# Which slots of a gather an expert's tokens take: dealt over eight groups of four, or filled in order

## The reference, cut to what matters

```python
scores = jax.nn.sigmoid((xf @ w_router).astype(jnp.float32))
...
_, top_idx = lax.top_k(jnp.where(expert_mask, sel_scores, -jnp.inf), TOP_K)
gates = jnp.take_along_axis(scores, top_idx, axis=-1)
gates = gates / gates.sum(-1, keepdims=True) * ROUTE_SCALE
...
hdn = jax.nn.silu(xb @ w_gate[e]) * (xb @ w_up[e])
return hdn @ w_down[e]
```

## Time and profile before

| | before |
|---|---|
| median of 3 runs (lowest, highest) | 1383.16 us (1380.08 to 1383.69) |
| the profiled execution's own time | 1383.16 us |
| its span in the profile | 1381.2 us |
| TensorE busy | 1340.4 us (97%) |
| SBUF loads and stores | 475.66 MB, 344 GB/s over the span |
| granted TensorE clock, mean | 0.993 of 2.4 GHz |

### The profile page before, as it was taken

How to read it: one execution, slowest core, us unless ns; L and a number is a source line. 1 busy time by engine, 2 the same in 40 slices (tenths; PEclk the granted TensorE clock), 3 DMA queues, 4 the chain that set the end, 5 groups by cost and what they waited for, 6 DMA issues and landing times.

```text
span 1381.2 us, 20332 instructions
## 1 busy us (share of the span) xinstructions
PE 1340.4 (97%) x7932; PEld 705.2 (51%) x7932; DVE 428.3 (31%) x1274; ACT 222.8 (16%) x551; POOL 356.9 (26%) x379
## 2 busy tenths in 40 slices
PE   8999999999999999999999999899999999999987
PEld 4755554455455455445447555454554545544443
DVE  0442563322322222222154424522223232232223
ACT  1154130111011010010121541201111111110001
POOL 2021345232232232222000212542322323222201
PEclk9999999999999999999999999999999999999999
DMA  9822468999999999999985224899999999999994
GB/s 330 327 94 90 153 232 318 423 418 421 421 421 418 422 422 421 420 422 421 414 290 200 91 109 154 304 377 420 420 417 421 421 420 419 422 422 420 421 425 194
DMA packets 92118, 475.66 MB, mean 344 GB/s; under 512 B 15165, under 2 KB 22553, under 8 KB 42769
## 3 DMA queue, kind: packets, MB, share of 16 engines
q1 hardware_dynamic: 76880, 442.73, 78.7%
q0 software_dynamic: 15168, 32.01, 6.4%
HBM read 491.21 MB, written 3.75 MB: 358 GB/s over the span
## 4 chain that ended last, share of the span: by engine, by line
PE 77%; SPq 10%; DMA 6%; DVE 3%; issue 1%; POOL 1%; ACT 1%; DVEq 0%; POOLq 0%; ACTq 0%
PE bank L692 26%; PE bank L721 13%; PE bank L661 13%; SPq L491 10%; PE bank L772 6%; DMA ring<-in_w_up_dram 5%; PE bank L783 5%; PE bank L999 3%; PE bank L894 1%; PE bank L657 1%; PE bank L1042 1%; PE bank L710 1%; PE bank L875 1%; PE bank L623 1%; PE bank L775 1%
## 5 line engine op out<-in xcount | busy, mean ns | idle before, releaser
L1985 POOL DMA_INDIRECT arena<-h_rows,rank_i x256 | 255.6, 999 | 608.0 <-DVE arena L1659 505.9
L692 PE MATMUL bank<-ring,arena 128*64 128x256 f32 x2784 | 314.9, 382 | 15.7 <-DMA ring<-in_w_up_dram 7.6
L692 PEld LDWEIGHTS bank<-ring,arena 128*64 128x64 f32 x2784 | 201.9, 138 | 139.0 <-issue 36.3
L661 PE MATMUL bank<-arena 128*128 128x512 f32 x512 | 247.1, 606 | 0.0
L1696 DVE TENSOR_TENSOR arena<-arena,bank 128x256 f32<-128x256 f32 x64 | 27.0, 421 | 560.6 <-ACT arena L1235 560.5
L721 PE MATMUL bank<-ring,arena 128*64 128x512 f32 x704 | 160.8, 598 | 0.0
L1640 DVE STREAM_TRANSPOSE arena<-arena 128x256 f32<-128x256 f32 x256 | 141.6, 610 | 25.9 <-DMA arena<-h_rows,rank_i 13.5
L692 PE MATMUL bank<-arena 128*64 128x256 f32 x1280 | 143.2, 379 | 3.0 <-DMA arena<-in_w_up_dram 1.9
L1240 ACT ACTIVATE arena<-bank 128x512 f32<-128x512 f32 x128 | 76.5, 597 | 430.4 <-PE bank L721 430.4
L661 PEld LDWEIGHTS bank<-arena 128*128 128x128 f32 x512 | 87.7, 191 | 88.9 <-issue 88.0
L692 PEld LDWEIGHTS bank<-arena 128*64 128x64 f32 x1280 | 91.7, 137 | 58.7 <-issue 10.3
(11 more groups left out here) (221 smaller groups left out, 904.4 us busy)
## 6 DMA issues: line engine op xcount, KB each, us to landing
ring<-in_w_up_dram SPq DMA_DIRECT2D x44, 2048.0 KB
ring<-in_w_down_dram SPq DMA_DIRECT2D x44, 2048.0 KB
ring<-in_w_gate_dram SPq DMA_DIRECT2D x43, 2048.0 KB
arena<-in_w_gate_dram SPq DMA_DIRECT2D x20, 2048.0 KB
arena<-in_w_up_dram SPq DMA_DIRECT2D x20, 2048.0 KB
arena<-in_w_down_dram SPq DMA_DIRECT2D x20, 2048.0 KB
ring<-in_w_in_dram SPq DMA_DIRECT2D x8, 2048.0 KB, 21.2
ring<-in_w_o_dram SPq DMA_DIRECT2D x4, 2048.0 KB, 11.9
```

The costliest lines, as they stand in the source:

```text
L661: last = mm(bank[SUM_BANKS[n][half]][0:w, :], selg[:, u, t0:t0 + w], y_sb[:, u, half * 512:(half + 1) * 512], start=False, stop=stop, skip ...
L692: last = mm(bank[5][64 * e:64 * e + 64, part * F:(part + 1) * F], xgT[:, u, kk, 64 * e:64 * e + 64], w[e][:, kk, :], start=(kk == 0), stop ...
L1985: pool.indirect_dma_start(out=xg[:, q % 2, b, :], out_offset=None, in_=h_rows, in_offset=bass.IndirectOffsetOnAxis(ap=rank_i[:, at:at + 1] ...
```

## The change

`eight`, the place to which MAX8 writes and from which MATCH_REPLACE8 reads, becomes the eight slots 8j to 8j + 7. An expert's tokens then fill its slots in order, 0 to 63. The view by groups goes. The number of instructions, of gathers and of rows stays.

```diff
                 for j in range(j0, j1):
-                    eight = list_groups[:, j // 4, ::(1, -1)[j // 4], j % 4]
+                    eight = mo["list"][0:64, 8 * j:8 * j + 8]
                     dve.max(eight, left).then_inc(list_step[l], 1)
                     hold_here(dve, list_step[l], r * (CAP // 4) + 2 * j + 1)
                     dve.match_replace(left, eight, left, 0.0).then_inc(list_step[l], 1)
...
-            list_groups = mo["list"][0:64, :].rearrange("p (h g i) -> p h g i", h=2, g=8)
...
                 for j in range(CAP // 8):
-                    eight = list_groups[:, j // 4, ::(1, -1)[j // 4], j % 4]
+                    eight = mo["list"][0:64, 8 * j:8 * j + 8]
                     dve.max(eight, left).then_inc(list_step[l], 1)
```

## The result

The change makes the kernel slower, by half of what was forecast: median 1389.25 us (6 runs, 1387.33 to 1394.24) against 1381.63 us (6 runs, 1379.51 to 1383.69), 7.6 us more. The ratio is 1.0056, 95% interval 1.0037 to 1.0076. The profiled execution took 1389.2 us with a span of 1387.2 us, 6.0 us over that of before.

The account below looks back on a forecast made before the run. Both layers were taken to end when the DMA engines have brought the last weights. Added rows on group 0's engines, 10.5 + 8.2 = 18.7 us, less 3.4, gave 15.3 us: 1383.2 to 1398.5 us, range 1391 to 1405.

Parts of the forecast that it names:

- The direction, the place and the mechanism: Slower, at both layers' ends: in-order slots give the engines of group 0 more gather rows, so their last weights come later.
- the sum: Both layers' ends: 10.5 us plus 8.2 us of added rows, less 3.4 us, makes 15.3 us slower.
- rows that count, both layers: Group 0's added rows after the queue fills: 242 less 20 in the first layer, 182 less 8 in the second.
- price of a row, as it reaches the end: DMA engine time per gathered row, from the queues' shares at 300 to 600 us: 47.2 ns.
- group 0's engines, longer: Engines bringing slots 0 to 3 of both halves: added rows lengthen their work by 10.5 and 8.2 us, together 18.7.
- how far they are ahead, both layers: Group 0's engines against the slowest engine at each layer's end: 1.7 us a layer, 3.4 together, taken off.
- the forecast's own case: Each engine has the same group of four slots in two quarters of the features: 1394 to 1403 us, chance 0.55.
- First wait at pair 23 and 21: TensorE's first wait for weights comes some 7 pairs sooner in the first layer and 3 sooner in the second.
- No fixed division: Gather packets go to engines in turn whatever their slots, so loads stay even: nothing measurable, 1383 us, chance 0.11.
- Neighbouring groups: Neighbouring groups of one quarter share an engine: 316 rows, 14.9 us less 3.4, so 1394.7 us; chance 0.22.
- Faster through relief of the slowest: Engines of groups 6 and 7 were the slowest and lose rows: up to 20.1 us faster, 1363 us; chance 0.02.
- Dearer through VectorE: Late rows also make TensorE wait for VectorE, 0.3 us over 40 pairs: 12 us more, 1411 us; chance 0.10.

Follow-up runs that it names:

- every slot filled: Kernel before, but slots without a token gather the row of token 271: 1416.47 us against 1378.58, and again 1417.78 against 1383.09.
- another pair of kernels: Kernel before with empty slots gathering token 271's row, only in group 0 (slots 0 to 3 of each half) or in all: 27.1 and 34.7 us slower.

## Why the prediction was wrong

**The direction, the place and the mechanism held.** Both layers end with the last weights (without a third of the loads the loss is gone); a packet is four slots; engines share the load by a fixed division, the same group in two quarters; VectorE's instructions take what they took before:

```profile
L1609 DVE MAX8 arena<-arena 64x8 f32<-64x272 f32 x8 | 3.5, 434 | 0.2
...
L1611 DVE MATCH_REPLACE8 arena<-arena 64x272 f32<-64x272 f32 x8 | 3.3, 417 | 0.0
```

434 and 417 ns against 440 and 418. The Trainium skill, DMA: Bandwidth & Descriptors, section The descriptor swizzle, puts a group's four quarters on two engines, and the two late engines bear it out. Its remark in the section Latency and other measured facts that engines 7 and 15 are usually slower is not borne out: with every slot filled all 16 finish the 89th load within 2.1 us.

**The step that failed is the sum**, 18.7 - 3.4 = 15.3 us, in three of its terms:

| term | forecast | by the runs |
|---|---|---|
| rows that count, both layers | 222 + 174 = 396 | 424 less 62 of the first four pairs = 362 |
| price of a row, as it reaches the end | 47.2 ns | 42 ns |
| group 0's engines, longer | 18.7 us | 15.2 us |
| how far they are ahead, both layers | 3.4 us | 7.6 us (5.1 by the traces) |
| the change | 15.3 us | 7.6 us |

The third line is 362 x 42 ns. The last, 15.2 - 7.6 = 7.6 us, is what the medians show, but the 7.6 us of credit come from another pair of kernels with intervals of some 3 us each, so the agreement to a tenth is luck. The traces of the change itself say much the same. From the 7th to the last load the first layer took 491.9 us before (196.7 to 688.6) and 497.0 after (195.8 to 692.8); from the third to the last load the second took 495.1 (867.6 to 1362.7) and 498.4 (870.3 to 1368.7). Of the 15.2 us of added rows 5.1 + 3.3 = 8.4 us reach the loads' end, which leaves a credit of 6.8 us.

The largest error is the fourth line: about 4 us of the 7.7. I bounded it by what fetches can do, 0 to 4 us a layer, and took 1.7; 3.4 to 3.8 a layer lie near the bound's end. The kernel before is not set by its mean engine but by the latest of 16: in its long stretches the last completion word of a load stands 0.9 to 1.8 us behind the mean one in the first layer and 1.3 to 3.5 us in the second. Two engines that are loaded on top start from somewhere in that field. What delays single engines stays open.

The price of a row came from dividing the queues' shares between packets and bytes. That found what a row adds to its own packet, 47 ns, and missed that a weight packet behind a gather's packet without rows takes some 17 ns longer, which a full packet spares. The first pairs I had cut at two; I now take four, which is an estimate.

**My range** of 1391 to 1405 left out 1389.25 because its low end joined at most 4 us of credit a layer with prices of 47 ns and more. A credit at that bound alone gives 18.7 - 8 = 10.7 us, 1393.9; in the forecast's own case only both errors at once reach 1389. A further 1.5 us came from the base: the forecast stood on 1383.16 us, and six runs of the kernel before gave 1381.63.

**Point by point of what I said the profile would show.** Packet counts: right to one record. Pace of 14.91 and 14.35: right. First wait at pair 23 and 21: it came at 27 and 23, late by the same errors. First layer's last pair 9 us later: 4.1. Second layer's experts 6.5 us longer: its first down products begin at 908.6 and 910.8 us, its last ones end at 1369.0 and 1375.0, so 3.8 us. DMA share below 1: right, 0.96 and 0.95. Not foreseen: the profiled executions differ by -0.5 us up to the first experts and by -1.9 us between the layers' experts; -0.5 + 4.6 - 1.9 + 3.8 is the 6.0 us of the spans. Where the 1.9 us come from is told below.

**The rivals.** No fixed division: out, by the completion words. Neighbouring groups: out, two engines are late and not four, although its 1394.7 lay nearer than my forecast. Faster through relief of the slowest: out by the result; and overloading from the top, where group 0 has the fewest rows and group 7 the most, is slower than before too. Dearer through VectorE: out, by the waits of line 692.

## What to carry to other kernels

A gather with absent rows still spreads by slot over fixed engines, so where lists are shorter than their slots, deal the entries over the engines; here, with 34 of 64 slots used and the engines full, that is worth 0.56%. When work is made uneven over engines that a big load shares, the price is (rows of the fullest engine) x (price of a row), less what that engine is ahead of the latest one: that credit cannot be taken from the mean. It has to be measured, as here by loading one group of slots alone and all together, and with enough runs: here it came out as 5 to 9 us. And the price of a row is what the whole queue loses by it, not only what its own packet takes: an entry that is absent still costs. Before the sum is trusted, ask also from which moment the queue is full, since nothing before it counts.

## What the runs showed of the hardware that I had not expected

Engines are independent to a degree I had not expected: two engines with 1.9 times the gather rows (1024 against about 545) end 16 to 20 us behind the others after 30 pairs and are neither helped nor hindered by them, within some 2 us of the runs in which all 16 have those rows.

A gather's packet that brings nothing takes 11 ns, but the weight packet behind it takes 329 ns in place of 312. With every slot filled a weight packet takes 310.9 ns on average from 300 to 600 us, against 313.2 ns before, so full packets cost the end less than their own durations say.

TensorE's granted clock differs between two executions in spells of a few microseconds behind a pause. After the first layer's norm, before and after the change (us, busy time, granted clock, DMA share, GB/s):

```profile
696.00:702.90 6.90, 4.72 (x23) 2.24 (x22) 5.68 (x16) 2.30 (x6) 1.13 (x2) 1.00 1.05 393
702.90:707.40 4.50, 4.40 (x7) 1.89 (x8) 3.00 (x9) 1.42 (x3) 0.54 (x1) 0.62 1.05 387
```

```profile
700.00:707.00 7.00, 4.86 (x24) 2.23 (x22) 5.64 (x15) 2.44 (x6) 1.13 (x2) 1.00 1.05 395
707.00:711.50 4.50, 4.36 (x16) 2.47 (x17) 3.04 (x9) 1.37 (x3) 0.54 (x1) 1.00 1.05 386
```

In the same 4.5 us TensorE finishes 7 matmul records at a granted clock of 0.62, most of the stretch at the lower of its two levels, and 16 at 1.00. TensorE had been idle for about two microseconds in the stretch ahead in both (4.72 of 6.9 and 4.86 of 7.0 us busy). The same eight products of line 772 take 592 to 1061 ns each in the one and 592 to 668 ns in the other, and from the start of the first to the start of the last 4.8 us (703.0 to 707.8) against 3.1 us (707.1 to 710.2). That is 1.7 us, and it is the larger part of the 1.9 us by which the changed kernel gained between the layers: a difference of this size between two single executions is not the change's.
